# A two-layer block on one core: packed score rows, merge inputs loaded at once, halves of merge units reordered, low weights moved to VectorE

## The chip, the cores and the metric

The kernel runs on one NeuronCore of one Trainium2 chip. The metric is the device time of one execution in microseconds. Three executions of the kernel before took 3519.25, 3522.42 and 3530.47 us; the median is 3522.42.

The names used below: PE is the tensor engine (its clock has two levels, and a granted clock of 1.00 in a profile is 2.4 GHz, 0.50 is 1.2 GHz), ACT is ScalarE, DVE is VectorE, POOL is GpSimd, SP is the engine from which nearly all DMAs are issued.

## The reference, cut to what matters

Two blocks follow each other on one sequence of 2048 tokens with 1024 channels. The first one is this; the second has the same outer form (normalise, project, an attention over a window of 128, a second branch, gates, merge, w_out, residual):

```
h = rms_norm(x, norm_g)
q, k, v, qi, ki, wi, z_a, u_b, z_b, gates = split(h @ w_in)
q, k = rope(rms_norm(q)), rope(rms_norm(k))          # 8 query heads, 2 key heads, 64 wide
allowed = key_chunk[None, :] <= q_chunk[:, None]     # a block of 128 queries sees the keys up to its chunk
idx = top_k(where(allowed, sum_h(relu(qi @ ki.T) * wi), -inf), 256)    # keys a query may use
p = softmax(q @ k[idx].T * scale); a = (p @ v[idx]) * silu(z_a)
b = multiscale_pool(u_b, pool_w, pool_scale) * silu(z_b)
g = sigmoid(gates + merge_bias)
y = g[:, :, 0] * (a @ w_branch_a) + g[:, :, 1] * (b @ w_branch_b)
x = x + y @ w_out
```

## The kernel before, in words

P is 128, T = 16 token tiles, D = 1024 = KD x P with KD = 8, BANK = 512 columns. All operands are float32. Where precision matters, a matrix is split into a high part (a copy rounded to fp32r, made by ACT) and a low part (raw minus high, made by DVE or POOL), and a product is three matmuls: high x high, high x low, low x high.

The program is a row of phases with a barrier between each two: `phase_tokens` (first layer), `phase_first` (projection and the choice of keys), `phase_attention`, `phase_pool`, `phase_output`, then for the second layer `phase_tokens`, `phase_second`, `phase_output`. In each phase every engine has its own list of instructions, written out in Python in the order in which the engine executes them; engines meet only through semaphores (`wait_ge`, `then_inc`). What stands behind a waiting instruction on the same engine waits too.

**Token phases.** `pipeline` (L268) runs the stages of all tiles, step u doing each stage for tile u minus its offset; after step 1 each engine does its part of splitting the weights, eight chunks k. ACT makes all highs (L563). DVE makes the lows of even k (L655), POOL those of odd k (L503). In the first layer DVE has the tables of angles (`angles`, L160 to L178) between its second and its third chunk, ACT the sines behind its highs; in the second layer ACT first copies a turned 128x512 matrix (L560). PE's first projection (L800) waits chunk by chunk for the lows.

**Attention.** A turn is one tile i of 128 queries and one of two key heads, with n = (i+1) x 128 keys and four heads r. PE makes scores in pieces of up to 512 keys (L1570), DVE adds the mask and takes the row maximum (L1491), ACT takes the exponential with its sum (L1549 is the copy of turned rows), DVE inverts (L1511), POOL multiplies each head's row by the inverse (L1470, one TENSOR_SCALAR per head), PE turns the rows 128 keys at a time (L1582) and multiplies by v (L1595). The score rows stand in `prob`, which has NPROB = 3 places for four heads with 2048 columns each; turn n takes place n % 3, and its scores wait until turn n-3 has been turned. The order of PE's work is worked out by `feeding`: step n is the n-th 128-key tile turned, and KEYS[turn] is the first step of a turn.

**Output phases.** The merge has 4 groups of 512 tokens (tg) and in each 8 units (dc, 128 output channels). A unit is 2 branches x 4 k x 3 matmuls (L1997 to L1999), 24 in all, into one of four PSUM tiles. Its sources `x = tg*8 + k` are loaded by SP through two slots `src`, split by ACT (L1929) and POOL (L1892) and kept in a ring of RING = 12 slots, so that the last four sources of a group wait until the previous group has been computed (`weighed`). Weights of the merge come in eight pieces through two slots in the end of yT (`load_split_weights`, L1749, L1755, L1761). After each unit DVE multiplies by the gates and adds (L1959). During the last eight units w_out is loaded piece by piece (each when its unit of the last group is finished) and split, and the product with w_out follows (L2014 to L2016).

## Time and profile before

| | us |
|---|---|
| three runs | 3519.25, 3522.42, 3530.47 |
| the profiled execution | 3526.29, of which the span 3524.3 |
| PE busy | 3203.7 (91%) |
| DVE, ACT, POOL busy | 1769.1, 1563.8, 1177.4 |
| tokens, first layer | 0.00 to 304.17 |
| projection and key choice | 304.17 to 1063.08 |
| attention | 1063.08 to 1517.26 |
| pool | 1517.26 to 1630.44 |
| output, first layer | 1630.44 to 2039.47 |
| tokens, second layer | 2039.47 to 2379.24 |
| second layer's middle | 2379.24 to 3113.26 |
| output, second layer | 3113.26 to 3524.30 |

The phase borders are read from the barriers. The names in a row: `o_` belongs to the output phases, `a_` to the attention, `t_` to the token phases, `p_` to the two large middle phases, `s_` to device memory. A row such as `L1892 POOL TENSOR_TENSOR o_in_lo<-o_src,o_in_hi 128x512 x32 | 43.7, 1372 | 135.9` says: 32 instructions of line 1892, 43.7 us in all, 1372 ns each, and 135.9 us in which the engine was idle before them.

### The profile page before, as it was taken

What the parts mean: (1) busy time and instruction counts of PE and PEld (TensorE: products, weight loads), DVE (VectorE), ACT (ScalarE), POOL (GpSimd) and SP (SyncE); (2) the same over time, 40 slices, a digit from 0 to 9 for tenths busy, and PEclk for the clock granted to TensorE, in tenths of its full rate; (3) what the DMA queues carried; (4) which work ended last, traced back from release to release, by engine and by line L of the source; (5) the groups of instructions that cost most, each with busy time, mean ns of one, the idle gap of its engine ahead of it and who ended that gap; (6) DMA issues with size and microseconds to landing.
All of it is one profiled execution on the core that took longest, in us unless ns stands there. A gap on an engine that the chain in (4) does not pass through costs nothing. (4 is left out here: it accounts for less than half of the span.)

```text
span 3524.3 us, 43474 instructions
## 1 busy us (share of the span) xinstructions
PE 3203.7 (91%) x15878; PEld 2632.4 (75%) x15878; DVE 1769.1 (50%) x3726; ACT 1563.8 (44%) x2454; POOL 1177.4 (33%) x790
## 2 busy tenths in 40 slices
PE   6996999799995999977899969988999999978999
PEld 6994888678873677765678858877888888856787
DVE  6775799888994666532331146652322232223332
ACT  3544688757963777711111023333544354421111
POOL 4440012001224999912222243322222222222222
PEclk9996999899996999967999979989999999989999
DMA  5666333343334211055553245536444633345522
GB/s 157 205 189 212 95 97 100 119 150 95 96 95 127 68 50 51 13 199 184 149 133 106 101 153 159 164 122 226 127 138 141 216 121 126 126 127 133 152 88 91
DMA packets 434157, 458.19 MB, mean 130 GB/s; under 512 B 30896, under 2 KB 318128, under 8 KB 432304
## 3 DMA queue, kind: packets, MB, share of 16 engines
q1 hardware_dynamic: 433968, 455.72, 41.8%
q8 instruction: 113, 1.85, 0.2%
q14 instruction: 76, 0.62, 0.1%
HBM read 289.70 MB, written 165.94 MB: 129 GB/s over the span
## 5 line engine op out<-in xcount | busy, mean ns | idle before, releaser
L1470 POOL TENSOR_SCALAR a_prob<-a_prob,a_inv 128x128 f32<-128x128 f32 (+15 forms) x128 | 384.2, 3030 | 81.9 <-DVE a_inv L1511 81.8
L1302 PE MATMUL p_pr<-p_hT,p_w_hi 128*128 128x512 f32 x896 | 355.5, 397 | 13.8 <-POOL p_w_lo L1085 9.9
L2390 PE MATMUL p_pr<-p_hT,p_w_hi 128*128 128x512 f32 x896 | 351.9, 393 | 16.3 <-DMA p_hT<-s_hT 16.3
L1303 PE MATMUL p_pr<-p_hT,p_w_hi 128*128 128x512 f32 x896 | 353.5, 395 | 0.0
L1304 PE MATMUL p_pr<-p_hT,p_w_lo 128*128 128x512 f32 x896 | 353.3, 394 | 0.0
L2391 PE MATMUL p_pr<-p_hT,p_w_hi 128*128 128x512 f32 x896 | 350.6, 391 | 0.0
L2392 PE MATMUL p_pr<-p_hT,p_w_lo 128*128 128x512 f32 x896 | 349.7, 390 | 0.0
L1085 POOL TENSOR_TENSOR p_w_lo<-p_w_raw,p_w_hi 128x256 fp32r<-128x256 f32 x144 | 108.0, 782 | 617.7 <-DVE p_level L1222 401.4
L800 PE MATMUL t_pj_ps<-t_w_hi,t_hT_slot 128*128 128x356 f32 (+2 forms) x768 | 271.9, 354 | 28.1 <-DVE t_w_lo L655 18.1
L1125 ACT ACTIVATE p_relu<-p_isc,p_level 128x2048 int8<-128x2048 f32 (+5 forms) x192 | 276.4, 1442 | 20.4 <-DVE p_level L1222 16.5
L1997 PE MATMUL o_b_ps<-o_in_hi,o_w_hi 128*128 128x512 f32 x512 | 214.6, 419 | 74.4 <-POOL o_in_lo L1892 44.3
L802 PE MATMUL t_pj_ps<-t_w_hi,t_hT_slot 128*128 128x356 f32 (+2 forms) x768 | 265.6, 346 | 0.0
L801 PE MATMUL t_pj_ps<-t_w_lo,t_hT_slot 128*128 128x356 f32 (+2 forms) x768 | 265.3, 345 | 0.0
L1491 DVE CUSTOM_DVE_ANT_0 a_prob<-a_s_ps,a_mask 128x512 f32<-128x512 f32 (+3 forms) x320 | 188.4, 607 | 152.1 <-PE a_s_ps L1570 148.2
L2237 POOL TENSOR_TENSOR p_w_lo<-p_w_raw,p_w_hi 128x1024 fp32r<-128x1024 f32 x56 | 136.3, 2434 | 329.4 <-ACT p_w_hi L2259 329.4
L1197 DVE TENSOR_SCALAR_CACHE_REDUCE p_ranks<-p_isc,p_level 128x1792 uint8<-128x1792 f32 (+4 forms) x130 | 223.0, 1753 | 2.6 <-DVE p_level L1204 0.4
L1570 PE MATMUL a_s_ps<-a_kT,a_qT 128*128 128x512 f32 (+3 forms) x640 | 198.3, 416 | 23.5 <-DMA a_kT<-s_kT 17.9
L1549 ACT ACTIVATE a_pt<-a_t_ps 128x512 f32<-128x512 f32 x272 | 153.6, 593 | 133.9 <-PE a_t_ps L1582 133.3
L1302 PEld LDWEIGHTS p_pr<-p_hT,p_w_hi 128*128 128x128 f32 x896 | 170.8, 191 | 53.2 <-POOL p_w_lo L1085 10.8
L2390 PEld LDWEIGHTS p_pr<-p_hT,p_w_hi 128*128 128x128 f32 x896 | 168.9, 188 | 55.2 <-issue 13.9
L1998 PE MATMUL o_b_ps<-o_in_lo,o_w_hi 128*128 128x512 f32 x512 | 209.8, 410 | 0.0
L1999 PE MATMUL o_b_ps<-o_in_hi,o_w_lo 128*128 128x512 f32 x512 | 209.1, 408 | 0.0
(276 smaller groups left out, 7117.1 us busy)
## 6 DMA issues: line engine op xcount, KB each, us to landing
p_w_raw<-in_w_in SPq DMA_DIRECT2D x112, 512.0 KB, 4.3
s_hT<-t_hT_slot SPq DMA_DIRECT2D x32, 1024.0 KB, 5.8
p_hT<-s_hT SPq DMA_DIRECT2D x64, 512.0 KB, 9.2
s_gT<-p_o_sb SPq DMA_DIRECT2D x128, 256.0 KB, 4.8
o_gates<-s_gT SPq DMA_DIRECT2D x64, 512.0 KB, 5.1
s_qT<-t_qT_slot SPq DMA_DIRECT2D x32, 512.0 KB, 2.7
s_zuT<-p_o_sb SPq DMA_DIRECT2D x64, 256.0 KB, 4.8
pl_wada<-in_w_ada SPq DMA_DIRECT2D x6, 2048.0 KB, 13.6
```

The costliest lines, as they stand in the source:

```text
L800: nc.tensor.matmul(o, hi, wh, start=(k == 0), stop=False)
L801: nc.tensor.matmul(o, hi, wl, start=False, stop=False)
L802: last = nc.tensor.matmul(o, lo, wh, start=False, stop=(k == KD - 1))
L1125: last = nc.scalar.activation(unread[:, o:o + w], isc[:, o:o + w], ACT.Sign, scale=-1.0, bias=level[:, b:b + 1], accum_out=counts[:, b:b + 1])
L1197: return nc.vector.tensor_scalar(unread[:].bitcast(mybir.dt.uint8)[:, at:at + w], isc[:, o:o + w], level[:, b:b + 1], None, op, ALU.add, a ...
L1302: nc.tensor.matmul(pr[n % NPR][:], wh, hi, start=(k == 0), stop=False)
L1303: nc.tensor.matmul(pr[n % NPR][:], wh, lo, start=False, stop=False)
L1304: last = nc.tensor.matmul(pr[n % NPR][:], wl, hi, start=False, stop=(k == KD - 1))
L1470: nc.gpsimd.tensor_scalar(prob[:, slot, 0:n], prob[:, slot, 0:n], inv[:, slot:slot + 1], None, ALU.mult).then_inc(normed, 1)
L2390: nc.tensor.matmul(pr[n % NPR][:], wh, hi, start=(k == 0), stop=False)
L2391: nc.tensor.matmul(pr[n % NPR][:], wh, lo, start=False, stop=False)
L2392: last = nc.tensor.matmul(pr[n % NPR][:], wl, hi, start=False, stop=(k == KD - 1))
```

## The change

1. **Token phases.** All eight lows are DVE's; POOL makes none, and does only masks or the band there. `pipeline` has a second hook, `later`, after step 2: the angle tables and sines of the first layer and the split of the turned matrix of the second stand there. The 44 TENSOR_SCALARs of the angles become two TENSOR_TENSORs with a table of frequencies that 44 memsets write at the kernel's start. PE turns the second layer's 128x512 matrix after its first projection instead of before.
2. **Attention.** `packed` puts several short turns into one place of `prob`, side by side (turns 0 to 6 in the first, 7 to 9, 10 and 11, 12 and 13, 14 and 15, then one each). Scores of the seven turns of the first place are issued four steps ahead of their turn, or at step 0. q and mask have three buffers, statistics have 64 columns. For the first eight turns there is one negation, one inversion and one POOL instruction for four heads; everywhere POOL's instruction is a TENSOR_TENSOR with the inverse spread along the row, in place of a TENSOR_SCALAR.
3. **Output phases.** `load_split_weights` is gone. The merge weights have a place of their own each and are all loaded at the start, as are the first 12 sources. All weight lows and four of the first eight source lows are DVE's. In each group PE computes units 0 to 3 whole, then the first branch of units 4 to 7 (a signal `branched` follows), then their second branch; a source that takes a slot of the first branch waits for `branched`, not for the group's end. yT is laid out by token tile.

The diff, cut to its core:

```diff
-        inv = inverse_frequencies()
-        for f in range(NF):
-            which = 0 if f < FREQS[0][1] + FREQS[1][1] else 1
-            last = nc.vector.tensor_scalar(ang[:, :, f], pos_f[:, which, :], inv[f], None, ALU.mult)
+        dve.wait_ge(freqs_ready, NF)
+        cut = FREQS[0][1] + FREQS[1][1]
+        for which, a, b in ((0, 0, cut), (1, cut, NF)):
+            last = nc.vector.tensor_tensor(ang[:, :, a:b], spread(pos_f[:, which, :], 2, b - a), spread(freqs[:, a:b], 1, T), ALU.mult)
         step(last)
...
         step(u)
         if u == 1 and weights:
             weights()
+        if u == 2 and later:
+            later()
...
-                for k in range(1, KD, 2):
-                    pool.wait_ge(w_hi_done, k + 1)
-                    nc.gpsimd.tensor_tensor(w_lo[:, k, :], w_raw[:, k, :], f32(w_hi[:, k, :]),
-                                            ALU.subtract).then_inc(w_lo_done[1], 1)
...
-                for k in range(0, KD, 2):
-                    if k == KD // 2 and not second:
-                        angles(dve)
+                for k in range(KD):
                     dve.wait_ge(w_hi_done, k + 1)
                     nc.vector.tensor_tensor(w_lo[:, k, :], w_raw[:, k, :], f32(w_hi[:, k, :]),
-                                            ALU.subtract).then_inc(w_lo_done[0], 1)
+                                            ALU.subtract).then_inc(w_lo_done, 1)
+
+            def setup_low():
                 if second:
                     dve.wait_ge(setup_pe, 2)
                     nc.vector.tensor_tensor(wsT[:, 1], pk_ps[:, 0:4, :], f32(wsT[:, 0]), ALU.subtract).then_inc(setup_pe, 1)
                 else:
+                    angles(dve)
                     rows(dve)
...
+    def packed():
+
+        out, b, col = [], 0, 0
+        for i, _ in TURNS:
+            n = (i + 1) * P
+            if col + n > SEQ:
+                b, col = b + 1, 0
+            out.append((b, col))
+            col += n
+        return out
+
+    BINS = packed()
+    FIRST = sum(b == 0 for b, _ in BINS)
+
+    def freed(turn):
+
+        b = BINS[turn][0] - NPROB
+        return KEYS[max(t for t in range(N_TURNS) if BINS[t][0] == b) + 1] if b >= 0 else 0
...
-            begin = KEYS[max(turn - NPROB + 1, 0)] + 1 if turn >= NPROB else 0
-            begin = max(begin, done)
+            begin = max(freed(turn) + 1 if freed(turn) else 0, done)
             end = max(KEYS[turn] - AHEAD, begin + 1)
             for x, (r, m) in enumerate(items):
                 step = begin + (end - begin) * x // len(items)
-                if turn < 2:
-                    step = 0
+                if turn < FIRST:
+                    step = max(KEYS[turn] - 4, 0)
                 scores_at[step].append((turn, r, m))
                 done = step
-                if m == len(pieces(i)) - 1:
-                    exps_at[min(step + 1, KEYS[turn]) if turn >= 2 else 0].append((turn, r))
-                    inverts_at[min(step + 2, KEYS[turn]) if turn >= 2 else 0].append((turn, r))
+                if m < len(pieces(i)) - 1 or (turn < BATCHED and r < REP - 1):
+                    continue
+                for q in range(REP) if turn < BATCHED else [r]:
+                    exps_at[min(step + 1, KEYS[turn])].append((turn, q))
+                inverts_at[min(step + 2, KEYS[turn])].append((turn, r))
...
                 n = (TURNS[turn][0] + 1) * P
-                head = turn * REP + r
-                slot = head % (NPROB * REP)
-                pool.wait_ge(inv_done, head + 1)
-                nc.gpsimd.tensor_scalar(prob[:, slot, 0:n], prob[:, slot, 0:n], inv[:, slot:slot + 1], None, ALU.mult
-                                        ).then_inc(normed, 1)
+                pool.wait_ge(inv_done, negations(turn, r))
+                if turn < BATCHED:
+                    (at, col), st = place(turn, 0), (turn * REP) % STATS
+                    p, f = prob[:, at:at + REP, col:col + n], spread(inv[:, st:st + REP], 2, n)
+                else:
+                    (at, col), st = place(turn, r), (turn * REP + r) % STATS
+                    p, f = prob[:, at, col:col + n], inv[:, st:st + 1].to_broadcast([P, n])
+                nc.gpsimd.tensor_tensor(p, p, f, ALU.mult).then_inc(normed, 1)
...
+                if turn < BATCHED:
+                    if r == REP - 1:
+                        dve.wait_ge(read, unit + 1)
+                        nc.vector.tensor_scalar(minus[:, st - r:st + 1], tops[:, st - r:st + 1, 0], -SCALE, None, ALU.mult
+                                                ).then_inc(negated, 1)
+                    return
...
+    ON_DVE = range(0, KD, 2)
...
-                if x >= 2:
-                    sp.wait_ge(lo_done, x - 1)
-                part = c.aT[k] if k < KB else c.bT[k - KB]
-                sp.dma_start(src[:, x % 2], part[:, cols]).then_inc(src_loaded[x % 2], 16)
+                if x >= RING + 2:
+                    wait_low(sp, x - 2)
+                branch = c.aT[k] if k < KB else c.bT[k - KB]
+                sp.dma_start(raw(x), branch[:, cols]).then_inc(raw_loaded[x] if x < RING else src_loaded[x % 2], 16)
...
-            load_src(0)
-            load_src(1)
-            sync(sp, range(0, 2))
-            for x in range(2, KD):
+            load_weights(0)
+            for x in range(KD):
                 load_src(x)
+            load_weights(1)
             load_gates(0)
+            load_weights(2)
             load_gates(1)
-            sync(sp, range(2, KD))
+            for n in range(3, KD):
+                load_weights(n)
+            for x in range(KD, RING):
+                load_src(x)
             for u in range(UNITS_ALL):
                 if u + 2 < UNITS_ALL:
                     load_gates(u + 2)
-                if u + KD < UNITS_ALL:
-                    load_src(u + KD)
+                if RING <= u + KD + 2 < UNITS_ALL:
+                    load_src(u + KD + 2)
...
+            high_weights(0)
             for x in range(GROUPS * KD):
-                if x == 2:
-                    scalar(act, range(0, 2))
                 if x == KD:
-                    scalar(act, range(2, KD))
-                act.wait_ge(src_loaded[x % 2], 16 * (x // 2 + 1))
-                if x >= RING:
-
-                    act.wait_ge(weighed, ((x - RING) // KD + 1) * KD)
-                nc.scalar.activation(in_hi[:, x % RING], src[:, x % 2], ACT.Copy).then_inc(hi_done, 1)
+                    for n in range(1, KD):
+                        high_weights(n)
+                if x < RING:
+                    act.wait_ge(raw_loaded[x], 16)
+                else:
+                    act.wait_ge(src_loaded[x % 2], 16 * ((x - RING) // 2 + 1))
+                    if (x - RING) % KD < KB:
+                        act.wait_ge(branched, (x - RING) // KD + 1)
+                    else:
+                        act.wait_ge(weighed, ((x - RING) // KD + 1) * KD)
...
+            low_merge(0)
+            for x in ON_DVE:
+                dve.wait_ge(hi_done, x + 1)
+                nc.vector.tensor_tensor(in_lo[:, x], raw(x), f32(in_hi[:, x]), ALU.subtract).then_inc(lo_done[0], 1)
+            for n in range(1, KD):
+                low_merge(n)
...
-            for u in range(UNITS_ALL):
+            def branch(u, half):
                 tg, dc = divmod(u, KD)
                 cols = slice(dc * P, (dc + 1) * P)
-                if tg == 0:
-                    ready(pe, dc)
-                if u >= 4:
-                    pe.wait_ge(multiplied, u - 3)
-                for k in range(KD):
-                    o, x = b_ps[u % 4][:, k // KB], tg * KD + k
+                if half == 0:
+                    if tg == 0:
+                        pe.wait_ge(w_lo_done, dc + 1)
+                    if u >= 4:
+                        pe.wait_ge(multiplied, u - 3)
+                for k in range(half * KB, (half + 1) * KB):
+                    o, x = b_ps[u % 4][:, half], tg * KD + k
                     if dc == 0:
-                        pe.wait_ge(lo_done, x + 1)
+                        wait_low(pe, x)
                     first, final = k % KB == 0, k % KB == KB - 1
                     nc.tensor.matmul(o, w_hi[:, k, cols], in_hi[:, x % RING], start=first, stop=False)
                     nc.tensor.matmul(o, w_hi[:, k, cols], in_lo[:, x % RING], start=False, stop=False)
                     last = nc.tensor.matmul(o, w_lo[:, k, cols], in_hi[:, x % RING], start=False, stop=final)
-                last.then_inc(weighed, 1)
+                return last
+
+            for tg in range(GROUPS):
+                for dc in range(KD - 4):
+                    branch(tg * KD + dc, 0)
+                    branch(tg * KD + dc, 1).then_inc(weighed, 1)
+                for dc in range(KD - 4, KD):
+                    last = branch(tg * KD + dc, 0)
+                last.then_inc(branched, 1)
+                for dc in range(KD - 4, KD):
+                    branch(tg * KD + dc, 1).then_inc(weighed, 1)
```

DVE's list at the start of the first token phase, before (t_w_lo are low weights, t_ang and t_turns the angle tables):

```order
L668 TENSOR_SCALAR t_xs<-t_x_in,t_rms 128x1024
L655 TENSOR_TENSOR t_w_lo<-t1r_w_raw,t_w_hi 128x1068 x2
L156 CAST t_pos_f<-t_pos_i 128x32
L160 TENSOR_SCALAR t_ang<-t_pos_f 128x16 x44
L167 TENSOR_SCALAR t_turns<-t_ang 128x704
L169 TENSOR_SCALAR t_turns<-t_turns 128x704
L171 SCALAR_TENSOR_TENSOR t_ang<-t_turns,t_ang 128x704 x3
L173 TENSOR_SCALAR t_ang<-t_ang 128x704
L176 SCALAR_TENSOR_TENSOR t_mirrored<-t_ang 128x704
L178 TENSOR_SCALAR t_mirrored<-t_mirrored 128x704
L655 TENSOR_TENSOR t_w_lo<-t1r_w_raw,t_w_hi 128x1068 x2
```

and after:

```order
L678 TENSOR_SCALAR t_xs<-t_x_in,t_rms 128x1024
L662 TENSOR_TENSOR t_w_lo<-t1r_w_raw,t_w_hi 128x1068 x8
L692 TENSOR_TENSOR t_h<-t_xT_ps,keep_gcol 128x1024
L678 TENSOR_SCALAR t_xs<-t_x_in,t_rms 128x1024
L162 CAST t_pos_f<-t_pos_i 128x32
L166 TENSOR_TENSOR t_ang<-t_pos_f,t_freqs 128x16x12
L166 TENSOR_TENSOR t_ang<-t_pos_f,t_freqs 128x16x32
```

The eight lows stand together, and the tables follow the first tile's h and the third tile's scaling.

PE's list at the start of the attention, before (a_s_ps are scores, a_t_ps rows turned 128 keys at a time, a_o_ps products with v):

```order
L1570 MATMUL a_s_ps<-a_kT,a_qT 128x128 x16
L1570 MATMUL a_s_ps<-a_kT,a_qT 128x256 x8
L1582 MATMUL a_t_ps<-keep_ident,a_prob 128x128 x8
L1570 MATMUL a_s_ps<-a_kT,a_qT 128x256 x8
L1582 MATMUL a_t_ps<-keep_ident,a_prob 128x128 x4
L1570 MATMUL a_s_ps<-a_kT,a_qT 128x384 x8
L1582 MATMUL a_t_ps<-keep_ident,a_prob 128x128 x4
L1595 MATMUL a_o_ps<-a_pt,a_v 64x256 x4
L1582 MATMUL a_t_ps<-keep_ident,a_prob 128x128 x4
L1570 MATMUL a_s_ps<-a_kT,a_qT 128x384 x8
L1582 MATMUL a_t_ps<-keep_ident,a_prob 128x128 x4
L1595 MATMUL a_o_ps<-a_pt,a_v 64x256 x4
```

and after:

```order
L1624 MATMUL a_s_ps<-a_kT,a_qT 128x128 x16
L1624 MATMUL a_s_ps<-a_kT,a_qT 128x256 x16
L1637 MATMUL a_t_ps<-keep_ident,a_prob 128x128 x8
L1624 MATMUL a_s_ps<-a_kT,a_qT 128x384 x8
L1637 MATMUL a_t_ps<-keep_ident,a_prob 128x128 x8
L1649 MATMUL a_o_ps<-a_pt,a_v 64x256 x4
L1637 MATMUL a_t_ps<-keep_ident,a_prob 128x128 x4
L1624 MATMUL a_s_ps<-a_kT,a_qT 128x384 x8
L1637 MATMUL a_t_ps<-keep_ident,a_prob 128x128 x4
L1649 MATMUL a_o_ps<-a_pt,a_v 64x256 x4
L1637 MATMUL a_t_ps<-keep_ident,a_prob 128x128 x8
L1649 MATMUL a_o_ps<-a_pt,a_v 64x256 x4
```

Before, 24 score matmuls (turns 0 to 2) stand ahead of the first turned rows; now 32 (turns 0 to 3) do, and turn 4's scores (128x384) come two turned tiles later.

SP's list at the start of the first output phase, before (o_yT is the place through which merge weights are loaded, o_src that of the sources):

```order
L1836 DMA o_src<-s_aT 128x512 x2
L1744 DMA o_yT<-in_w_branch_a 128x4x128
L1744 DMA o_yT<-in_w_branch_b 128x4x128
L1744 DMA o_yT<-in_w_branch_a 128x4x128
L1744 DMA o_yT<-in_w_branch_b 128x4x128
L1836 DMA o_src<-s_aT 128x512 x2
L1836 DMA o_src<-s_bT 128x512 x4
L1842 DMA o_gates<-s_gT 128x2x512 x2
L1744 DMA o_yT<-in_w_branch_a 128x4x128
L1744 DMA o_yT<-in_w_branch_b 128x4x128
```

and after (r_w_raw and r_in_raw are the new places of the same):

```order
L1869 DMA r_w_raw<-in_w_branch_a 128x4x128
L1869 DMA r_w_raw<-in_w_branch_b 128x4x128
L1865 DMA r_in_raw<-s_aT 128x512 x4
L1865 DMA r_in_raw<-s_bT 128x512 x4
L1869 DMA r_w_raw<-in_w_branch_a 128x4x128
L1869 DMA r_w_raw<-in_w_branch_b 128x4x128
L1876 DMA o_gates<-s_gT 128x2x512
L1869 DMA r_w_raw<-in_w_branch_a 128x4x128
L1869 DMA r_w_raw<-in_w_branch_b 128x4x128
L1876 DMA o_gates<-s_gT 128x2x512
```

Before, the first two sources and two pieces of weights go first, and six sources follow, each behind an earlier one's split; now one piece of weights and then eight sources go without a wait.

## Rows read from the trace of the kernel before

**Rows 1.** Windows by phase: stretch us, length, engines' busy (instructions), PEclk, DMA share, GB/s.
```profile
1063.08:1517.26 454.18, 410.77 (x2816) 303.28 (x2816) 246.75 (x1056) 303.08 (x529) 384.24 (x129) 0.95 0.19 59
1630.44:2039.47 409.03, 368.30 (x1536) 296.86 (x1536) 100.03 (x89) 53.69 (x64) 98.65 (x55) 0.93 0.43 124
3113.26:3524.30 411.04, 368.72 (x1536) 296.90 (x1536) 131.93 (x105) 69.93 (x96) 110.72 (x87) 0.92 0.43 123
```

**Rows 2.** Waits of PE, whole span: waiting line <- releaser: us, times, mean.
```profile
PE o_b_ps L1997 <- POOL o_in_lo L1892: 44.3, 26, 3.2
...
PE o_b_ps L1997 <- DVE o_w_lo L1755: 26.1, 2, 13.6
PE a_t_ps L1582 <- POOL a_prob L1470: 23.4, 6, 5.5
...
PE t_pj_ps L800 <- DVE t_w_lo L655: 18.1, 3, 14.2
```

**Rows 3.** Windows in the merges of both output phases.
```profile
1639.05:1855.91 216.86, 191.62 (x767) 151.72 (x768) 73.59 (x68) 32.80 (x45) 60.26 (x38) 0.90 0.54 144
...
1639.05:1698.42 59.37, 51.36 (x193) 39.53 (x193) 18.66 (x17) 12.83 (x17) 23.87 (x14) 0.83 0.58 161
1698.42:1752.79 54.37, 47.61 (x193) 37.97 (x192) 16.30 (x17) 5.05 (x8) 10.76 (x8) 0.91 0.50 132
1720.15:1752.79 32.64, 32.64 (x145) 27.03 (x144) 12.27 (x12) 2.53 (x4) 5.16 (x4) 1.00 0.51 131
3122.26:3337.60 215.34, 192.34 (x767) 151.66 (x768) 72.76 (x68) 33.55 (x45) 60.53 (x39) 0.90 0.56 145
```

**Rows 4.** Timeline, start of the first output phase: start, length, engine, line, [idle before].
```profile
1630.44 0.81 SPq L1836 DMA_DIRECT2D o_src<-s_aT  x2
...
1637.77 1.23 DVE L1755 TENSOR_TENSOR o_w_lo<-o_yT,o_w_hi 128x1024 fp32r<-128x1024 f32 x1 [8.38 <-ACT o_w_hi L1749]
...
1646.06 0.63 ACT L1929 ACTIVATE o_in_hi<-o_src 128x512 fp32r<-128x512 f32 x1 [5.01 <-DMA o_src<-s_bT]
```

**Rows 5.** Lines by form, 1630 to 1861: busy, mean ns | idle before.
```profile
L1892 POOL TENSOR_TENSOR o_in_lo<-o_src,o_in_hi 128x512 fp32r<-128x512 f32 x32 | 43.7, 1372 | 135.9 <-ACT o_in_hi L1929 135.9
...
L1929 ACT ACTIVATE o_in_hi<-o_src 128x512 fp32r<-128x512 f32 x32 | 20.0, 630 | 165.0 <-DMA o_src<-s_aT 100.3 <-PE o_b_ps L1999 32.4 <-DMA o_src<-s_bT 32.3
...
L1749 ACT ACTIVATE o_w_hi<-o_yT 128x1024 fp32r<-128x1024 f32 x8 | 8.5, 1060 | 20.1 <-DMA o_yT<-in_w_branch_b 20.1
```

**Rows 6.** Timeline, a boundary between two merge groups.
```profile
1704.20 0.33 SPq L1836 DMA_DIRECT2D o_src<-s_bT  x1
...
1709.30 0.63 ACT L1929 ACTIVATE o_in_hi<-o_src 128x512 fp32r<-128x512 f32 x1 [4.21 <-DMA o_src<-s_bT]
```

**Rows 7.** Windows in the attention.
```profile
1072.10:1180.00 107.90, 77.50 (x420) 56.20 (x421) 58.16 (x310) 54.85 (x139) 68.20 (x49) 0.81 0.30 94
1180.00:1497.00 317.00, 316.31 (x2258) 235.26 (x2257) 187.75 (x744) 238.24 (x374) 316.04 (x80) 1.00 0.15 44
```

**Rows 8.** Lines by form, whole span: POOL's normalising in both layers.
```profile
L1470 POOL TENSOR_SCALAR a_prob<-a_prob,a_inv 128x1024 f32<-128x1024 f32 x8 | 22.6, 2852 | 0.0
...
L1470 POOL TENSOR_SCALAR a_prob<-a_prob,a_inv 128x2048 f32<-128x2048 f32 x8 | 43.4, 5445 | 0.0
...
L2243 POOL TENSOR_TENSOR p_prob<-p_prob,p_inv 128x1024 f32<-128x1024 f32 x30 | 56.8, 1894 | 182.7 <-DVE p_inv L2328 182.7
```

**Rows 9.** Token phases: timeline of the first; two lines (ns min/median/max) and timeline, second.
```profile
14.42 11.74 POOL L503 TENSOR_TENSOR t_w_lo<-t1r_w_raw,t_w_hi 128x1068 fp32r<-128x1068 f32 x4
...
21.43 8.13 DVE L160 TENSOR_SCALAR t_ang<-t_pos_f 128x16 f32<-128x16 f32 x44
...
35.53 2.45 DVE L655 TENSOR_TENSOR t_w_lo<-t1r_w_raw,t_w_hi 128x1068 fp32r<-128x1068 f32 x2
...
L503 POOL TENSOR_TENSOR t_w_lo<-t2r_w_raw,t_w_hi x4: 3059/4147/4167, 2060.3 to 2071.5; 128x1280 fp32r<-128x1280 f32 x4
...
L655 DVE TENSOR_TENSOR t_w_lo<-t2r_w_raw,t_w_hi x4: 1493/3742/4202, 2059.1 to 2068.7; 128x1280 fp32r<-128x1280 f32 x4
...
2057.28 0.60 ACT L560 ACTIVATE t_wsT<-t_pk_ps 128x512 fp32r<-128x512 f32 x1 [5.13 <-PE t_pk_ps L779]
```

237 lines of the change are left out of this document (123 added, 114 removed).

## The prediction

> **What bounds the kernel now.** I read in this order: the page's engine shares, the windows of each phase (the phases are separated by barriers, so each one's time simply adds to the others'), the list of what TensorE (PE) waits for, and then, in the phases that the change touches, the windows of their parts and the timeline of their first microseconds. The reader is to see three things. First, PE is the busiest engine of the changed phases, with 368.3 us of 409.0 in the first output phase, 368.7 of 411.0 in the second, 410.8 of 454.2 in the attention [rows 1]; so only what makes PE idle, or run at the lower of its two clocks (granted 0.50, 1.2 GHz, against 1.00, 2.4 GHz), can be won. Second, the idle time has few causes: pieces of low source on POOL 44.3 us, two waits for low merge weights 26.1, POOL's normalised rows 23.4 in six waits, low weights of the token phases 18.1 in three [rows 2]. Third, these idle times stand beside a granted clock under 1 (0.83 in the first merge group, 0.81 in the attention's start), so that a stall costs more than its own length.
>
> **Output phases, twice.** A merge is 32 units of 24 matmuls. In a stretch without a stall six units take 32.64 us [rows 3], 5.44 each, so 32 take 174.1. The first merge takes 216.86 and the second 215.34 [rows 3]: 42.8 and 41.2 us too long, 84 together. In the first, 15.9 stand in its first group (59.37 less 8 x 5.44 = 43.5) and 10.9 in the second (54.37 less 43.5); the other two hold the remaining 16.
>
> The first group: before, SP issues two sources, then weights through two slots, so that a piece of weights is only loaded when an earlier one is split, and the sources come in two at a time as well: ScalarE (ACT) waits 100.3 us for s_aT and 32.3 for s_bT [rows 5], and a source is still being split at 1646.06, seven microseconds after PE began [rows 4]. After, all is loaded at once. The first low weight piece is ready at about the same time (1637.77 + 1.23 = 1639.0 before; its loads now stand first in the queue, so I take half a microsecond off). ACT splits the eight sources in 8 x 0.63 = 5.0 us and POOL makes four lows in 4 x 1.37 = 5.5 [rows 5], VectorE (DVE) the other four beside it. So unit 0, which starts cold and takes some 8 us at the lower clock against 5.44, hides most of it: excess 3 instead of 15.9. The seven other weight pieces need 1.06 each on ACT [rows 5] and 1.23 on DVE [rows 4] against 5.44 per unit: hidden. Should DMA deliver the first pieces too slowly, PE finds them late and up to the whole 13 us is lost again.
>
> The three boundaries: a group's last four sources can be split only when the previous group has read their ring slots; then two loads wait one after another for lows. In the row at 1704.20 SP issues such a load 5.8 us after the group's start (1698.42), ACT takes it at 1709.30, 5.1 us later [rows 6], POOL 1.4 after that: it is ready some 12 us in, where PE wants it 4 to 5 us in. After, PE has read the slots four half units (4 x 2.72 = 10.9 us) before the group ends. I place the last source's low at 4.3 to 5.0 us into the next group, where PE wants it at 4.8: 0 to 1 us for each boundary instead of 8 to 11.
>
> The passage to w_out gets worse by 1 to 2 us: the last four units end in a row, so DVE and SP release w_out's pieces 4 to 7 later (before, one comes free every 5.44 us, now every 2.72, with a splitting chain of about 1.1 + 1.2 us behind each).
>
> Sum for one phase: 12.9 + 27 of 42.8 less what is left at boundaries (about 1.5) = 38.5, less 1.5 = 37; 74 for both. Bounds: 30 (source chain half a unit later than I place it) to 43 (all excess gone), so 60 to 86.
>
> **Attention.** From 1180.00 to 1497.00 PE is busy 316.3 us of 317.0 at clock 1.00 [rows 7]: its work is unchanged, so nothing is won or lost there while PE stays the bound. All of the gain is in 1072.10 to 1180.00: 77.5 us busy of 107.9, clock 0.81 [rows 7]. At full clock without a stall that would be 77.5 x 0.81 = 63, so 45 at the most. Before, turn n's scores go out when turn n-3 has been read, so PE waits for POOL's normalising six times, 23.4 us [rows 2]. After, sixteen small turns share five bins and the scores of turns 0 to 3 go out at once: the first wait (5.5, the mean) stays, the other five (18) go. Of the clock's shortfall, some 107.9 x 0.19 = 20, the part at the phase's start stays, since the loading and the first chain stay; I take 6 back. 18 + 6 = 24. Bounds 10 (new waits for POOL, busy 68.2 us of this stretch, take half) and 40 (45 less the first wait). The third q and mask buffer moves two loads (q, mask) ahead on SP; they are small and stand behind the first keys.
>
> POOL's normalising changes from TENSOR_SCALAR to TENSOR_TENSOR with a column spread over the row. POOL is busy 316.0 us of the 317 [rows 7]: it is the second bound there, and this price matters. TENSOR_SCALAR takes 2852 ns at 128x1024 and 5445 at 128x2048; the same form as the new one, in the second layer (L2243), takes 1894 at 128x1024 [rows 8]; one with two full inputs takes 1372 at 128x512 [rows 5], 2.68 ns a column against 2.79 for TENSOR_SCALAR. The nearest row is L2243's, so I take 0.66 of the present price (POOL's 384 us of the phase [rows 1] become some 255); from both sides 0.66 to 0.96. Either way POOL falls below PE and nothing is gained on PE's side.
> The Trainium skill (GPSIMD Engine Reference, 4.1 Engine selection) speaks against this edit: it says that one-input operations on GpSimd run at about line rate and two-input ones about twice slower than VectorE's. By that rule the new form would cost up to twice the old one. The trace disagrees: L2243's row is a third cheaper than TENSOR_SCALAR at the same shape.
>
> **First tokens.** The projection waits for the last low weights, 35.53 + 2.45 = 37.98 us. Before, DVE makes two, runs the tables (44 TENSOR_SCALARs from 21.43 on and more after them) and then the last two; POOL needs 11.74 us for its four (2.94 each) [rows 9]. DVE alone needs 1.23 each (2 in 2.45). After: a first low at about 14.5, when POOL's piece on h has ended, and eight at the pace of ACT's highs, 1.2 each, 24.0. The first projection begins 14.0 us earlier; the load of a later x takes back 1: gain 13, bounds 9 to 15. The tables now come behind, before the first heads; they need about 7.5 us (two instructions for 44, the rest as before), with a dozen microseconds of projection over them; without that cover they would cost up to 4, hence the 9.
>
> **Second tokens.** Lows before: 2059.1 to 2071.5 + 4.17 = 2075.7, DVE and POOL taking 4.2 and 4.15 when side by side, 1.49 when DVE is alone [rows 9]. After: ACT's highs no longer wait for the copy at 2057.28 [rows 9], the first low starts at about 2055.1, and 8 x 1.49 = 11.9 later, 2067.0, the last ends. 8.7, of which I take 8.5; bounds 5 (ACT's highs set the pace from 2057) to 10.
> The Trainium skill (SBUF — State Buffer, "SBUF: two separate sides") says that a VectorE operation with two SBUF inputs and a GpSimd operation exclude each other. The trace agrees: 1.49 alone, about 4.2 side by side. By that rule taking POOL away costs nothing; if both had run freely at their own prices, four on each engine would have ended as early as eight on DVE, and the move alone would give nothing.
>
> **Sum.** 74 + 24 + 13 + 8.5 = 119.5. The profiled execution took 3526.3 us: 3406.8. The median of the runs, 3522.4, lies 3.9 below that execution: 3403. All lower bounds together (60 + 10 + 9 + 5 = 84) give 3438, all upper ones (86 + 40 + 15 + 10 = 151) 3371.
>
> **Rivals.**
> B. The attention's start gains only about 5: ACT's copies of transposed rows queue behind a whole row of exponentials, DVE's maxima behind one another, so PE finds the next turn as late as before. For it: DVE and ACT are busy 58 and 55 us of 108 there, and work of eight turns is issued together. Against it: neither is near full. 3422.
> C. The boundaries stay: the loads of a group's last two sources stand on SP behind the gates of units 6 and 7, which wait for sums that now come late. For it: my place for the last source has no margin. Six boundaries x 8 us = 48 lost: 3451.
> E. The merges' first groups stay as they are since DMA delivers seven megabytes no faster (161 GB/s is drawn there already [rows 3]): 2 x 13 back, 3429.
> D. Slower than before: the new form on POOL is dearer, not cheaper. POOL, full now, would set the time from 1180 on: each per cent costs 3.2 us, and from +30% (about 7.1 us for 128x2048 instead of 5.45) it eats the other 95 us. At twice the price, +316 - 96 = +220: 3742. Against it stands L2243's row; for it only that in-place rows of this phase were never run in this form.
> F. The change doesn't do what it says: the waits only change their names, within 0.3% of 3522.
>
> **How the numbers follow.** Forecast 0.68, B 0.12, C 0.10, E 0.05, D 0.03, F 0.02. The forecast's own range is 3385 to 3420. The range 3375 to 3438 takes in B and E and the lower bounds, and leaves out C, D, F and a little of the upper side. A measurement of this kernel can tell about 0.3% (10.6 us) from no change. All but D and F are faster by more: 0.95; F 0.02; D 0.03.
>
> **What would show it.** In the profile after: both merges at 180 to 190 us, with the granted clock at 1.00 from the second unit on and no wait for POOL's low sources above 1 us at a boundary (C: waits of some 8 at the second half of a group's first unit; E: the first group near 59); the attention's steady part still 100% PE with POOL at about two thirds, and its start some 24 us shorter (B: 5); POOL's 128x1024 rows near 1.9 us (D: over 3.7); the last low weight at 24 us, and in the second tokens 8.7 us earlier than now after the phase's start. Wrong would be any phase outside these five that moves by more than 2 us, or a sum under 84.

## The result, and the profile after

The changed kernel takes 3410.1 us (median of four, 3408.45 to 3413.96) against 3522.1 (four, 3519.25 to 3530.47): ratio 0.9681, 95% interval 0.967 to 0.9693, 112 us less. The forecast was 3403, 119 less. The profiled execution, 3413.96, is the slowest of its four; its span is 3412.2.

The five changed phases in the windows of the changed kernel (stretch, length, busy time of PE, PEld, DVE, ACT, POOL, clock, DMA share, GB/s; three of them answer to [rows 1]):

```profile
0.00:294.81 294.81, 254.85 (x1616) 245.00 (x1616) 198.20 (x479) 133.45 (x204) 123.10 (x125) 0.95 0.59 181
...
1055.29:1484.31 429.02, 404.01 (x2816) 299.77 (x2816) 236.15 (x976) 302.98 (x529) 250.50 (x105) 0.95 0.20 63
...
1597.54:1974.67 377.13, 355.89 (x1536) 291.76 (x1536) 110.08 (x97) 53.55 (x64) 86.48 (x47) 0.97 0.45 134
1974.67:2302.26 327.59, 293.29 (x1668) 251.83 (x1668) 196.10 (x297) 122.23 (x202) 117.62 (x148) 0.94 0.49 159
...
3035.21:3412.20 376.99, 355.06 (x1536) 291.14 (x1536) 143.21 (x113) 69.79 (x96) 98.46 (x79) 0.97 0.45 134
```

| part | forecast gain | before, us | after, us | gain |
|---|---|---|---|---|
| first tokens | 13 | 304.17 | 294.81 | 9.4 |
| attention | 24 | 454.18 | 429.02 | 25.2 |
| first output | 37 | 409.03 | 377.13 | 31.9 |
| second tokens | 8.5 | 339.77 | 327.59 | 12.2 |
| second output | 37 | 411.04 | 376.99 | 34.1 |
| the three others together | 0 | 1606.1 | 1606.7 | -0.6 |
| sum | 119.5 | 3524.3 | 3412.2 | 112.1 |

What PE waits for now (us in all, times, longest). It answers to [rows 2], whose third number is the longest wait of its group too, not the mean as the heading there has it:

```profile
PE o_b_ps L2050 <- DVE o_in_lo L2003: 22.4, 2, 11.7
...
PE o_b_ps L2077 <- POOL o_w_lo L1932: 8.9, 2, 5.1
PE a_t_ps L1637 <- POOL a_prob L1518: 8.4, 3, 3.5
PE t_pj_ps L808 <- DVE t_w_lo L662: 5.6, 6, 2.1
PE o_b_ps L2050 <- POOL o_in_lo L1926: 5.1, 7, 1.2
PE t_pj_ps L808 <- POOL t_hT_slot L524: 3.7, 2, 2.6
```

The reader is to see four things. First, POOL's low sources cost 5.1 us in seven waits, where they cost 44.3 in 26. Second, the first line is no loss of the merge: it is the time before its first matmul, once in each output phase, which stood under DVE's o_w_lo before (26.1). Third, the wait for POOL's low pieces of w_out, 8.9 us in two, was not among the waits before; it is the price of the new order. Fourth, in the first tokens two waits for POOL's t_hT_slot have come up, 3.7 us.

### The profile page after: what moved, and what is told of

It is laid out like the page before. It is cut to its first block and busy times, and to the rows that moved or that the text cites. A ratio compares the mean times of both kernels' runs of the same rounds, so it can differ in the third digit from the quotient of the medians.

```text
span 3412.2 us, 43258 instructions
## 1 busy us (share of the span) xinstructions
PE 3171.1 (93%) x15878; PEld 2617.5 (77%) x15878; DVE 1775.7 (52%) x3672; ACT 1563.3 (46%) x2454; POOL 999.2 (29%) x742
## 5 line engine op out<-in xcount | busy, mean ns | idle before, releaser
L1518 POOL TENSOR_TENSOR a_prob<-a_prob,a_inv 128x1024 f32<-128x1024 f32 (+12 forms) x104 | 250.5, 2419 | 188.6 <-DVE a_inv L1563 188.4
L2050 PE MATMUL o_b_ps<-o_in_hi,o_w_hi 128*128 128x512 f32 x512 | 203.3, 397 | 27.7 <-DVE o_in_lo L2003 22.4
L1312 PEld LDWEIGHTS p_pr<-p_hT,p_w_hi 128*128 128x128 f32 x896 | 171.3, 191 | 52.4 <-POOL p_w_lo L1095 10.5
L2077 PE MATMUL o_b_ps<-o_w_hi,o_in_hi 128*128 128x512 f32 x512 | 201.4, 393 | 10.1 <-POOL o_w_lo L1932 8.9
L2051 PE MATMUL o_b_ps<-o_in_lo,o_w_hi 128*128 128x512 f32 x512 | 201.8, 394 | 0.0
```

The costliest lines, as they stand in the source:

```text
L1312: nc.tensor.matmul(pr[n % NPR][:], wh, hi, start=(k == 0), stop=False)
L1518: nc.gpsimd.tensor_tensor(p, p, f, ALU.mult).then_inc(normed, 1)
L2077: nc.tensor.matmul(o, y_hi[:, s, k], wh, start=(k == 0), stop=False)
```

## The experiments

A comparison within one phase, taken from single profiled executions, has a scatter. With the changed kernel's code in the phase, the first tokens took 294.6 to 295.7 us in eight executions, the attention 426.6 to 429.0 in nine (429.0 is the changed kernel's own), the first output phase 374.5 to 378.8 in six, the second tokens 326.6 to 329.4 in ten; the first output phase of before took 409.0, 405.5 and 404.8 in three. Smaller differences than these say nothing. Totals are medians.

**The three parts, each alone on the kernel before.** Edit of e1: the functions `constants`, `pipeline` and `phase_tokens` of the change; of e2: `phase_attention`; of e3: `phase_output`. As a diff against the changed kernel, for e1:

```diff
-def phase_attention(c, stack):    # with packed places
+def phase_attention(c, stack):    # as before
-def phase_output(c, stack, second):    # all loaded at once, halves reordered
+def phase_output(c, stack, second):    # as before
```

> The kernel before with the token part of the change alone (all low weights on DVE, tables and sines later, angles in two instructions). The profile of the change has the first token phase 9.4 us shorter and the second 12.2 us. Theory (each part's gain is its own, the barriers separate them): 21.6 us less than before, 3500 to 3501; first token phase 294.8, second 327.6. Rival (part of the second token phase's gain comes from the shorter phase in front of it, through the clock): only 17 to 18 less, second token phase 331 or more.

> The kernel before with the attention part alone. Theory: 25.2 us less, 3497, attention 429.0 us, all other phases as before. Rival (the gain of the phase is partly that of what runs ahead of it): 15 to 20 less.

> The kernel before with the output part alone. Theory: 31.9 + 34.1 = 66.0 us less, 3456; output phases 377 us each. Rival (parts overlap, or the chip's state differed between the two profiled executions): 60 or less, or over 72.

Measured beside 3523.8 for the kernel before: e1 3500.2 (ratio 0.9936, 0.9919 to 0.9952), first tokens 294.6, second 329.0. e2 3496.4 (0.9922, 0.9906 to 0.9939), attention 427.4. e3 3458.6 (0.9815, 0.9799 to 0.9831), first output phase 374.6. The gains, 23.7, 27.4 and 65.2, add to 116.3; together they gave 112 to 114. Each part's gain is its own; e1 and e3 came in at the theory's figures, e2 two better. What is beyond additive is 2 to 4 us, about what the executions scatter.

**POOL's instruction in the attention.** e4:

```diff
-                p, f = prob[:, at, col:col + n], inv[:, st:st + 1].to_broadcast([P, n])
-                nc.gpsimd.tensor_tensor(p, p, f, ALU.mult).then_inc(normed, 1)
+                p = prob[:, at, col:col + n]
+                nc.gpsimd.tensor_scalar(p, p, inv[:, st:st + 1], None, ALU.mult).then_inc(normed, 1)
```

> The changed kernel, but POOL normalises the rows of turns 8 to 31 by TENSOR_SCALAR again, one head each, as before. Before, POOL and PE were both busy 316 of 317 us. Theory PE (PE is the bound there and POOL only kept up): POOL has some 384 us of work in a phase 429 us long, of which about 14 are over before it starts and 19 follow its last row, so it is full from the start; attention 429 to 434, total 3410 to 3415. Rival POOL (POOL's cheaper form gave the gain): the attention falls back towards 445 to 454 us, total 3426 to 3435.

Measured 3408.8 (3406.4 to 3409.4), the changed kernel's time within its scatter, 1 us under the range of theory PE and far from the 3426 to 3435 of theory POOL. The edit reaches turns 8 to 31 alone; the first eight turns keep one TENSOR_TENSOR for four heads. Windows of the steady part, first of the changed kernel, then of e4:

```profile
1172.10:1464.11 292.01, 291.45 (x2090) 216.99 (x2088) 170.67 (x673) 219.23 (x339) 189.69 (x68) 1.00 0.13 40
```

```profile
1172.10:1464.11 292.01, 291.07 (x2085) 216.21 (x2084) 170.16 (x671) 218.64 (x339) 291.07 (x70) 1.00 0.13 40
```

POOL is busy 189.69 us of 292.01 in the one, 291.07 in the other, and PE is at its limit in both. So PE was the bound and POOL only kept up in these turns; the cheaper form frees a third of POOL and gives no time there. What it gives in the first eight turns no run shows. The two prices, in the changed kernel and in e4 (busy, mean ns):

```profile
L1518 POOL TENSOR_TENSOR a_prob<-a_prob,a_inv 128x1024 f32<-128x1024 f32 x10 | 18.7, 1893 | 11.0 <-DVE a_inv L1563 11.0
```

```profile
L1518 POOL TENSOR_SCALAR a_prob<-a_prob,a_inv 128x1024 f32<-128x1024 f32 x8 | 22.6, 2850 | 0.0
```

**The order of the halves.** e5 has whole units in all groups:

```diff
-            for tg in range(GROUPS):
-                for dc in range(KD - 4):
-                    branch(tg * KD + dc, 0)
-                    branch(tg * KD + dc, 1).then_inc(weighed, 1)
-                for dc in range(KD - 4, KD):
-                    last = branch(tg * KD + dc, 0)
-                last.then_inc(branched, 1)
-                for dc in range(KD - 4, KD):
-                    branch(tg * KD + dc, 1).then_inc(weighed, 1)
+            for u in range(UNITS_ALL):
+                branch(u, 0)
+                branch(u, 1).then_inc(weighed, 1)
...
-                    if (x - RING) % KD < KB:
-                        act.wait_ge(branched, (x - RING) // KD + 1)
-                    else:
-                        act.wait_ge(weighed, ((x - RING) // KD + 1) * KD)
+                    act.wait_ge(weighed, ((x - RING) // KD + 1) * KD)
```

> The changed kernel with PE's old order in the merges: every unit whole, and a group's last four sources wait for the whole previous group. Theory (the order of the halves is what removes the boundary stalls): the first two of these sources are split 2.0 and 3.4 us into the group, the loads of the other two wait for those lows and take some 5 us, so their lows are ready at about 9 and 10 where PE wants them at 4.1 and 4.8; 5 us of waiting and 2 to 3 at the lower clock at each of six boundaries, against 1.1 now, less some 3 at each passage to w_out: 3435 to 3448. Rival (loading twelve sources and all weights at once is enough, the order gives nothing): boundaries within 1 us of now, passages shorter, 3402 to 3406.

Measured 3450.1 (3448.6 to 3452.8), 40 us above the changed kernel and 2 above the range of the theory. PE's waits in it:

```profile
PE o_b_ps L2046 <- POOL o_in_lo L1925: 36.8, 12, 4.1
...
PE o_b_ps L2067 <- DVE o_w_lo L1989: 3.0, 3, 1.8
```

Twelve waits, two at each of six boundaries, 6.1 us for each boundary, where the changed kernel has 5.1 over the whole of both merges. Behind each boundary of the first merge the granted clock is 0.50 for 7 to 10 us:

```profile
1657.30:1664.10 6.80, 4.87 (x12) 3.38 (x11) 3.61 (x4) 1.26 (x2) 3.01 (x2) 0.50 0.71 210
1708.50:1718.70 10.20, 7.09 (x16) 5.11 (x17) 3.83 (x4) 1.89 (x3) 3.52 (x4) 0.50 0.62 170
1763.10:1769.90 6.80, 3.74 (x10) 2.49 (x9) 3.36 (x4) 2.52 (x3) 5.01 (x3) 0.50 0.57 175
```

The passage to w_out, on the other hand, costs 3.0 for both phases instead of 10. So the order of the halves alone is worth 40 us. The other 26 of the output part's 66 are left by difference for the loading at once with the lows on DVE, which was not run by itself.

**The last group whole.** e6:

```diff
             for tg in range(GROUPS):
-                for dc in range(KD - 4):
+                whole = KD if tg == GROUPS - 1 else KD - 4
+                for dc in range(whole):
                     branch(tg * KD + dc, 0)
                     branch(tg * KD + dc, 1).then_inc(weighed, 1)
+                if whole == KD:
+                    continue
```

> The changed kernel, but in the fourth group, behind which no sources follow, the units are computed whole. Theory (units 4 to 7 ending close together make w_out's last pieces late; PE waits 5.5 and 4.6 us there, before the change 1.6 and 1.8): 3 to 4 us less in each output phase, 3402 to 3405. Rival (the waiting comes from the gates' loads or from DVE, not from the order): no change, 3409 to 3411.

Measured 3398.8 (3396.0 to 3400.2; ratio to before 0.964, 0.9625 to 0.9655), 11 us less than the change and 3 us below the range of the theory, though the mechanism is the one expected. Waits in it:

```profile
PE o_b_ps L2050 <- POOL o_in_lo L1926: 4.6, 7, 1.0
...
PE o_b_ps L2080 <- DVE o_w_lo L1993: 2.5, 4, 1.0
```

The 8.9 us for POOL's o_w_lo are gone, and with them a stretch at the lower clock. Windows of the passage, the changed kernel's and e6's:

```profile
1794.00:1800.80 6.80, 4.72 (x11) 3.71 (x12) 3.06 (x2) 2.12 (x2) 2.03 (x1) 0.50 0.45 157
1787.00:1810.00 23.00, 17.54 (x67) 13.63 (x65) 8.64 (x8) 5.30 (x5) 4.74 (x2) 0.85 0.53 158
```

```profile
1787.00:1810.00 23.00, 21.94 (x95) 17.51 (x95) 5.08 (x5) 3.18 (x3) 4.15 (x2) 1.00 0.28 101
```

In 23 us PE gets through 95 matmuls in place of 67. The two output phases became 5.5 and 5.0 us shorter. How the wait comes about shows in the changed kernel's timeline: a unit ends every 2.7 us there, DVE's product waits for its gates, and the w_out pieces of the late units arrive late:

```profile
1791.12 1.22 DVE L2010 TENSOR_TENSOR o_gates<-o_b_ps,o_gates 128x1024 f32<-128x1024 f32 x1 [1.13 <-DMA o_gates<-s_gT]
...
1792.55 1.06 ACT L1976 ACTIVATE o_w_hi<-r_w_raw 128x1024 fp32r<-128x1024 f32 x1 [3.81 <-DMA r_w_raw<-in_w_out]
...
1793.68 2.34 POOL L1932 TENSOR_TENSOR o_w_lo<-r_w_raw,o_w_hi 128x1024 fp32r<-128x1024 f32 x1 [14.79 <-ACT o_w_hi L1976]
...
1796.08 0.80 PE L2077 MATMUL o_b_ps<-o_w_hi,o_in_hi 128*128 128x512 f32 x1 [5.07 <-POOL o_w_lo L1932]
```

**POOL's lows back in the token phases.** e7:

```diff
-                for k in range(KD):
+                for k in range(0, KD, 2):
                     dve.wait_ge(w_hi_done, k + 1)
...
             def setup_masks():
+                for k in range(1, KD, 2):
+                    pool.wait_ge(w_hi_done, k + 1)
+                    nc.gpsimd.tensor_tensor(w_lo[:, k, :], w_raw[:, k, :], f32(w_hi[:, k, :]),
+                                            ALU.subtract).then_inc(w_lo_done[1], 1)
```

> The changed kernel, but POOL makes the low weights of odd k in both token phases again, DVE those of even k; tables stay behind. Theory of exclusion (the two engines' operations take turns): first phase 4 x (1.25 + 2.4) = 14.6 us for the lows instead of 11.0, second 4 x 4.15 = 16.6 instead of 13.3; +7 in all, 3415 to 3419. Rival (they run beside each other): 4 x 2.44 = 9.8 and 4 x 3.06 = 12.2, no change or 2 less, 3408 to 3411.

Measured 3415.9 (3409.4 to 3417.7), 5.7 above the change. The lows (ns min/median/max, first and last start), POOL's line and DVE's, and behind them DVE's line in the changed kernel:

```profile
L506 POOL TENSOR_TENSOR t_w_lo<-t1r_w_raw,t_w_hi x4: 3476/3484/3490, 14.3 to 24.6; 128x1068 fp32r<-128x1068 f32 x4
L506 POOL TENSOR_TENSOR t_w_lo<-t2r_w_raw,t_w_hi x4: 4144/4152/4177, 1985.1 to 1997.4; 128x1280 fp32r<-128x1280 f32 x4
...
L666 DVE TENSOR_TENSOR t_w_lo<-t2r_w_raw,t_w_hi x4: 3127/4191/4211, 1983.3 to 1994.6; 128x1280 fp32r<-128x1280 f32 x4
```

```profile
L662 DVE TENSOR_TENSOR t_w_lo<-t1r_w_raw,t_w_hi x8: 1255/1258/2549, 12.9 to 22.7; 128x1068 fp32r<-128x1068 f32 x8
L662 DVE TENSOR_TENSOR t_w_lo<-t2r_w_raw,t_w_hi x8: 1478/1570/3125, 1988.2 to 2000.0; 128x1280 fp32r<-128x1280 f32 x8
```

Side by side the two engines take 3.48 or 4.15 us each for what DVE alone does in 1.26 or 1.57: they take turns, and a pair is worth 3.5 us against 2.5. That is exclusion as predicted. The second tokens show it in their time, 334.2 us against 327.6. The first tokens hardly do: 0.9 us more, 295.7, as long as in other executions with the changed kernel's token code (294.6 to 295.7). There the lows end 4.2 us later (28.1 us against 23.9) and the second tile's projection starts 4.7 later, the third tile's (53.8 against 51.3) only 2.5, the packing 1.4: the changed kernel gives its lead back in the waits for POOL's t_hT_slot behind the tables, which e7 does not have. So in the first tokens at least 8.5 of the 9.4 us stay without the lows on DVE, and are left to the moved and shortened tables; in the second 6.6 of the 12.2 come from the lows.

**The tables earlier.** e8:

```diff
             def scaled(t, slot, used):
+                if not second and isinstance(t, int) and t == 2:
+                    angles(dve)
                 done(dve, "rms_done", t)
...
                 else:
-                    angles(dve)
                     rows(dve)
```

> The changed kernel, but DVE computes the angles in front of the third tile's scaling, where it waits for a load for 7.8 us, instead of behind it. Theory (the tables behind the scaling keep DVE from the third tile's h, and PE waits 2.6 and 1.8 us for it): these two waits go, the first projection comes up to 2.4 us later; 0 to 3 us less, 3407 to 3410. Rival (the wait at the second projection comes from POOL's own order): it stays and 2 are lost, 3412.

Measured 3404.5 (3402.5 to 3409.3), 5.7 less than the change and 2.5 below the range of the theory, with the first tokens 4.1 us shorter in its profile (290.8 us). PE's waits for POOL's t_hT_slot are one of 1.1 us instead of two of 3.7. That alone is no proof: in e4, whose token phases are the changed kernel's, the same single 1.1 stands, and its first tokens took 295.5, for the clock fell to 0.50 at 35.4 us there and PE came to its third projection only at 52.3. What is e8's own is that PE's third projection starts at 50.1 us instead of 51.3 (51.8 in e1) and the fourth at 64.9 instead of 67.2. These 2.3 us last to the phase's end. The other 1.8 come up in its last 90 us, where the granted clock is 0.91 in e8 and 0.86 in the changed kernel; no run ties them to the edit.

**The old issue order in the attention.** e9 (packed places and batched small instructions stay):

```diff
-            begin = max(freed(turn) + 1 if freed(turn) else 0, done)
+            begin = KEYS[max(turn - NPROB + 1, 0)] + 1 if turn >= NPROB else 0
+            begin = max(begin, done)
...
-                if turn < FIRST:
-                    step = max(KEYS[turn] - 4, 0)
+                if turn < 2:
+                    step = 0
```

> The changed kernel, but PE's scores in the attention are issued in the old order (turn n's after turn n-3 has been turned), with the places packed and one negation, inversion and normalising per turn for the first eight turns as in the change. Theory (the earlier issue removes the waits): most of the 25 us come back, attention 445 to 454, total 3426 to 3435. Rival (the batched small steps shorten each turn's chain, the issue order matters little): attention 429 to 437, total 3410 to 3418.

Measured 3423.9 (3422.1 to 3424.6 in three of its four executions; the other took 13982 us and is not in the range), 13.8 above the change; attention 438.2 against 429.0 and, before, 454.2. That lies between both expectations. The waits for POOL's rows in e9:

```profile
PE a_t_ps L1638 <- POOL a_prob L1519: 13.1, 6, 3.6
```

Before they were 23.4 in six [rows 2], in the changed kernel 8.4 in three. What e9 keeps cuts them from 23.4 to 13.1 over the same six, the earlier issue cuts their number. In phase time what e9 keeps is worth 16.0 of the 25.2 us, the earlier issue 9.2 (11 against the 427.5 us that the attention took in most executions). Where these stand can be read from the turns. Turn 8 starts its turned rows 86.9 us after the phase's start before, 71.3 in e9 and 69.9 in the changed kernel; from there to turn 17 it is 97.0, 96.8 and 89.1. So 15.6 of e9's 16.0 us are won in the eight turns that the batching covers, and the earlier issue gives its time mainly in turns 8 to 16. Batching is not the only thing in those eight turns, though: POOL's new form is cheaper too (1038 ns for 128x512, where four TENSOR_SCALARs at 128x128 took 604 each and one at 128x512 took 1564), and q and mask have a third buffer. No run parts these three.

**Who makes the first sources' lows.** e10 `ON_DVE = ()`, e11 `ON_DVE = range(KD)`:

```diff
-    ON_DVE = range(0, KD, 2)
+    ON_DVE = ()
```

> The changed kernel, but POOL makes the lows of all first eight sources in the merges (1.26 us each alone) and DVE none. In the change each takes 1.7 us on both engines while they meet, 8.7 us from first to last. Theory of exclusion: POOL alone needs 8 x 1.26 = 10.1 us, 1 to 2 more per phase, 3411 to 3414. Rival (half the work on each engine is worth its nominal half, 5 us): 8 to 10 more, 3418 to 3420.

> The changed kernel, but DVE makes the lows of all first eight sources (0.69 us each alone, ACT's highs come every 0.63). Theory of exclusion: the last low is ready some 2.5 us earlier, of which PE, at its lower clock in the first unit, can use 1 to 2: 2 to 4 less in both phases, 3406 to 3408. Rival (PE's first unit is set by its clock alone): no change, 3410.

Measured 3414.4 (3413.1 to 3417.6) and 3411.6 (3408.0 to 3415.6). POOL alone costs 4.3 more, just above the 3411 to 3414 of the theory and under the 3418 of its rival; the first unit ends 20.6 and 18.6 us after the start of the two output phases, against 17.2 and 16.8 in the changed kernel. For DVE alone the total did not move, so its theory (3406 to 3408) failed and its rival's 3410 is what came out. The first unit took 7.66 us in place of 10.46, but that is no gain of the edit: with the changed kernel's own sources it took 7.4 to 10.5 in twelve output phases of six executions (7.55 in e4), and ended 15.1 to 17.2 us after the phase's start, where e11 has 15.1 in both. So the sharing between the two engines costs 0 to 2 us a phase, and the totals do not tell it from nothing. Timeline of the changed kernel, where the two engines share the work (the phase starts at 1597.54):

```profile
1605.06 4.47 ACT L1971 ACTIVATE o_in_hi<-r_in_raw 128x512 fp32r<-128x512 f32 x7 [1.64 <-DMA r_in_raw<-s_aT]
...
1605.77 6.33 POOL L1926 TENSOR_TENSOR o_in_lo<-r_in_raw,o_in_hi 128x512 fp32r<-128x512 f32 x4 [33.57 <-ACT o_in_hi L1971]
...
1606.34 4.62 DVE L2003 TENSOR_TENSOR o_in_lo<-r_in_raw,o_in_hi 128x512 fp32r<-128x512 f32 x3 [2.19 <-ACT o_in_hi L1971]
```

DVE's three take 1.54 each, where its first alone took 0.69.

**The three together.** e12 has the edits of e6, e8 and e11.

```diff
+                whole = KD if tg == GROUPS - 1 else KD - 4
...
+                if not second and isinstance(t, int) and t == 2:
+                    angles(dve)
...
+    ON_DVE = range(KD)
```

> The changed kernel with the last merge group whole, the angle tables before the third tile's scaling and the first sources' lows all on DVE. If the gains add: 11.3 from the first, 5.7 from the second, 2 to 4 from the third, 3389 to 3392. Rival (two of them fill the same waits): 3396 to 3399.

Measured 3398.9 (3395.3 to 3399.8; ratio to before 0.9643, 0.963 to 0.9656), the same as e6 alone. That is the rival's figure, but not by shared waits: e11's part had nothing to add, and the tables' gain of e8 did not come back: in e12's profile PE waits 2.7 us for DVE's scaling of the third tile (0.3 in e8 and in the changed kernel), the clock falls to 0.50 at 36 us, and the first tokens are only 0.7 us shorter than in the changed kernel. The scaling beside POOL's split of h, first in e8, then in e12:

```profile
33.85 0.76 DVE L679 TENSOR_SCALAR t_xs<-t_x_in,t_rms 128x1024 f32<-128x1024 f32 x1 [1.52 <-POOL t_rms L519]
33.94 2.87 POOL L524 TENSOR_TENSOR t_hT_slot<-t_h,t_hT_slot 128x1024 fp32r<-128x1024 f32 x1
```

```profile
33.13 2.92 DVE L679 TENSOR_SCALAR t_xs<-t_x_in,t_rms 128x1024 f32<-128x1024 f32 x1 [0.71 <-POOL t_rms L519]
33.15 2.35 POOL L524 TENSOR_TENSOR t_hT_slot<-t_h,t_hT_slot 128x1024 fp32r<-128x1024 f32 x1
```

The two start within 0.1 us of each other, and one of them is drawn out: POOL's in e8 (and in the changed kernel, 2.87 us), DVE's in e12 (2.92 instead of 0.76). Of the fourteen kept traces e12's is the only one in which DVE's is, so the gain of e8 can be lost to a race of two engines that the edit does not settle. Why POOL's went first this once stays open. e6 is the version to keep: one edit, 11 us under the change and some 125 under the kernel before.

## Why the prediction was right

The time of 3410 lies 7 us above the forecast of 3403, inside the range; B, C, D, E and F did not occur. Part of the closeness is luck: the first tokens and the two output phases gave 11.6 us less than their terms, the attention and the second tokens 4.9 more. By its steps:

- *Boundaries of the merge.* Predicted 0 to 1 us each, one of 1.5 for three together; measured 1.5, 1.0 and 0.9 too long in the first merge, 3.4. Right mechanism, and e5 shows it: without the new order 6.1 us of waiting at each. What is left of C are seven short waits in both merges, the longest 1.2 us, where C had 8 at each boundary and the forecast none above 1.
- *First group.* Excess predicted 3; measured 5.0 and 4.2 in the two merges (the first unit 0 takes 10.46 us instead of 5.44), and 2.6 to 4.7 in e3, e4, e7, e8 and e9 with the same code, so that the 3 was about right. I had counted DVE's four lows as beside POOL's, and they take turns (1.5 to 1.7 us for each low); but e11, where DVE makes all, still has 4.3 and 3.4 of excess, so this is not shown to be its cause. PE began 6.75 us after the phase's start instead of 8.61, 1.9 better where I took 0.5 (6.5 to 8.3 in the other executions). E (DMA too slow) was wrong: DMA moved 343 GB/s in that unit, twice what the merge before drew:

```profile
1604.29:1614.75 10.46, 9.28 (x24) 6.90 (x25) 6.37 (x5) 6.50 (x9) 6.33 (x4) 0.58 1.04 343
```

- *The passage to w_out.* The step that was mis-sized: "worse by 1 to 2 us". PE waited 5.5 and 4.6 us there instead of 1.6 and 1.8, and the clock fell behind it; e6 gave 5.5 and 5.0 us back in the two phases. From the phase's start to the first w_out matmul the first output phase gained 36.5 (225.7 to 189.2, forecast 38.5), and lost 4.6 behind it (forecast 1.5); the second gained 37.1 and lost 3.1.
- *Attention.* 24 forecast, 25.2 measured, but for reasons of which one was missing, so that the closeness of this term is luck. I gave all to the earlier issue and priced the batching of small instructions, and POOL's cheaper form on them, at nothing; e9 shows 9.2 from the first and 16.0 from the rest of the part. Three waits of 8.4 us in all are left, where the first alone was to stay, so that the waits gave 15.0 instead of 18; the 5.5 taken for "the first wait (5.5, the mean)" is the longest of the six, their mean is 3.9, and the term should have read 19.5. The clock's term was 6, and PE's busy time for the same 2816 matmuls fell by 6.8 (410.77 to 404.01). That the steady part would not move is shown by e4, and from the start of turn 17 to that of turn 31 it is 249.7 us before and 249.5 after.
- *POOL's price.* 0.66 of the old one at 128x1024, as taken from the second layer's row: 1893 ns against 2852 [rows 8]. The Trainium skill (GPSIMD Engine Reference, 4.1 Engine selection) would have had the two-input form dearer; the runs show the opposite, and D fell with it. e4 adds that in turns 8 to 31 even TENSOR_SCALAR's price would have cost nothing.
- *First tokens.* The first half came as computed: the second tile's projection started at 35.90 us (49.94 less the 14.0 is 35.94; the lows' end was forecast at 24.0 and measured at 23.9). But the tables behind it were priced as hidden by a dozen microseconds of projection, and they were not: the third tile's projection waits 2.6 us for POOL's split of h, and the packing 1.8 more, which left 9.4 of 13. The lower bound of 9, with "up to 4" for tables without cover, is what came.
- *Second tokens.* 12.2 instead of 8.5. The lows ended 26.8 us after the phase's start instead of 36.2, 9.4 earlier. In e7, where POOL makes half of them again, they end 32.2 us after the phase's start, so 5.4 of the 9.4 are exclusion, and the other 4.0 go with the earlier start of ACT's highs (first low at 13.5 us instead of 19.6). Of the 2.8 of the phase's gain beyond these 9.4 some 1.5 is clock: the second tile's projection took 15.8 us instead of 17.3, at 1.00 throughout.

## What to carry to other kernels

Behind most stalls of PE that this study removed, the records show a stretch at half clock, so that a wait cost more than its own length (e5: 25.8 us of waiting more than in the changed kernel over both output phases, 40 us of time; e6: 7.5 us less, 10.5 us of time). An edit that trades one wait for a later one should be applied only where the first wait exists: the reordered halves pay in three groups and cost in the fourth. And when a change holds a large part and a cheap-looking small one (here one instruction for four in the short turns, in a cheaper form), measure the small one as well: here what e9 kept gave 16.0 us against the large part's 9.2. A single profile in which a wait has gone is not yet a gain: in e4 it went without any edit to that phase, and the first unit of the merge varies by 3 us between executions of the same code.
